# Reordered loads and step sizes at the start of a hybrid decoder step, and a reordered router

## The reference

```python
hp = rmsnorm(xp, norm_mix[i])
proj = h @ w_in                       # z | x, B, C | dt_raw
xbc = silu(conv(concat(conv_state, xbc)) + conv_b)       # width 4, per channel
dt = softplus(dt_raw + dt_bias); a = -exp(a_log)
y, h_last = ssd_scan(xs, dt, a, bm, cm, ssm_state)       # cumulative sums of dt * a over tokens
y = rmsnorm((y + xs * d_skip) * silu(z)) ; x = x + y @ w_out
...
grp = argmax(t @ w_route_group)                          # then the top 2 of the group's 8 experts
act = silu(gate) * up * combine ; out = out + act @ w_down
```

## Time and profile before

| | us |
|---|---|
| median of 3 runs | 1652.96 (1651.39 to 1654.72) |
| the profiled execution | 1652.1 |
| its span (first to last instruction) | 1650.3 |
| TensorE busy in the span | 1601.2 (97%) |
| VectorE busy | 619.9 (38%) |
| ScalarE busy | 449.0 (27%) |
| GpSimd busy | 142.2 (9%) |
| HBM traffic over the span | 328 GB/s |

### The profile page before, as it was taken

How to read it: one execution, slowest core, us unless ns; L and a number is a source line. 1 busy time by engine, 2 the same in 40 slices (tenths; PEclk the granted TensorE clock), 3 DMA queues, 4 the chain that set the end, 5 groups by cost and what they waited for, 6 DMA issues and landing times.

```text
span 1650.3 us, 21196 instructions
## 1 busy us (share of the span) xinstructions
PE 1601.2 (97%) x7929; PEld 934.2 (57%) x7929; DVE 619.9 (38%) x1356; ACT 449.0 (27%) x1168; POOL 142.2 (9%) x295
## 2 busy tenths in 40 slices
PE   9998879999999999999999999999999999999997
PEld 7877667653444344344877888877653444344342
DVE  4589993321322222123023544554421322222123
ACT  3488872211111111112143142232311111111112
POOL 1233341100000000001001202230000000000000
PEclk9999989999999999999999999999999999999999
DMA  9668777499999999999434956696599999999995
GB/s 340 204 212 264 219 237 286 151 400 401 427 428 424 429 428 424 430 425 399 175 132 162 331 183 239 173 275 285 226 401 402 429 426 425 429 427 426 430 424 214
DMA packets 107589, 542.24 MB, mean 329 GB/s; under 512 B 8780, under 2 KB 33556, under 8 KB 78546
## 3 DMA queue, kind: packets, MB, share of 16 engines
q1 hardware_dynamic: 90518, 485.20, 73.0%
q0 software_dynamic: 16672, 55.53, 10.7%
q10 hardware_dynamic: 316, 0.37, 0.1%
HBM read 524.81 MB, written 16.45 MB: 328 GB/s over the span
## 4 chain that ended last, share of the span: by engine, by line
PE 78%; DVE 10%; DMA 5%; ACT 4%; issue 2%; POOL 0%; SPq 0%; DVEq 0%; ACTq 0%
PE bank L1049 25%; PE bank L1413 14%; PE bank L1061 13%; PE bank L1032 5%; PE bank L1055 4%; PE bank L884 4%; DMA ring<-in_moe_w_gate_up 3%; PE bank L1344 3%; PE bank L1316 3%; DVE arena L2452 2%; PE bank L1642 2%; DVE arena L2297 2%; PE bank L1075 1%; ACT arena L1764 1%; DVE arena L2460 1%
## 5 line engine op out<-in xcount | busy, mean ns | idle before, releaser
L1049 PE MATMUL bank<-ring,arena 128*64 128x512 f32 x1520 | 335.7, 592 | 2.9 <-DMA ring<-in_moe_w_gate_up 2.8
L1413 PE MATMUL bank<-hT,ring 128*128 128x264 f32 x1152 | 269.4, 389 | 0.2
L1413 PEld LDWEIGHTS bank<-hT,ring 128*128 128x128 f32 x1152 | 214.4, 190 | 41.2 <-issue 3.9
L1049 PEld LDWEIGHTS bank<-ring,arena 128*64 128x64 f32 x1520 | 111.7, 137 | 214.4 <-issue 214.1
L2297 DVE TENSOR_TENSOR arena<-arena,bank 128x512 f32<-128x512 f32 x32 | 34.2, 1070 | 389.2 <-ACT arena L1764 389.2
L1061 PE MATMUL bank<-ring,arena 128*64 128x512 f32 x768 | 170.1, 595 | 1.6 <-DVE arena L2218 1.6
L1055 PE MATMUL bank<-arena 128*128 128x512 f32 x256 | 127.0, 618 | 1.6 <-ACT arena L1774 1.6
L1764 ACT ACTIVATE arena<-bank 128x512 f32<-128x512 f32 x32 | 19.1, 597 | 386.0 <-PE bank L1049 386.0
L2244 DVE SCALAR_TENSOR_TENSOR arena<-arena 128x1024 f32<-128x1024 f32 x32 | 41.1, 1284 | 213.2 <-ACT arena L1774 213.2
L1049 PE MATMUL bank<-arena 128*64 128x512 f32 x512 | 112.6, 592 | 0.0
L1061 PEld LDWEIGHTS bank<-ring,arena 128*64 128x64 f32 x768 | 53.8, 137 | 101.8 <-issue 99.7
(11 more groups left out here) (348 smaller groups left out, 1713.2 us busy)
## 6 DMA issues: line engine op xcount, KB each, us to landing
ring<-in_moe_w_gate_up SPq DMA_DIRECT2D x78, 2048.0 KB, 18.6
ring<-in_moe_w_down SPq DMA_DIRECT2D x48, 2048.0 KB, 23.6
arena<-in_moe_w_gate_up SPq DMA_DIRECT2D x32, 2048.0 KB, 18.9
ring<-in_attn_qkv SPq DMA_DIRECT2D x18, 2048.0 KB, 11.6
ring<-in_moe_w_gate_up SPq DMA_DIRECT2D x34, 1024.0 KB, 17.6
arena<-in_moe_w_down SPq DMA_DIRECT2D x32, 1024.0 KB, 21.2
ring<-in_ssm_in_proj SPq DMA_DIRECT2D x10, 2048.0 KB, 14.2
out<-arena POOLq DMA_DIRECT2D x24, 512.0 KB, 4.3
```

The source lines that it names most:

```text
L1049: mm = pe.matmul(bank[j][e * SLOTS:(e + 1) * SLOTS, :], Xg[:, 4 * half + k, 2 * (p % 2) + e, :], gate_rows(2 * half + e, p, k, first)[:, j ...
L1413: mm = pe.matmul(bank[i % 2][:, 0:T], wv[:, k, (i % 4) * P:(i % 4 + 1) * P], hT[:, k, :], start=(n == 0), stop=(n == DT - 1))
```

## The change

In the beginning: GpSimd's copy of old rows goes behind the first `old_columns`; ScalarE asks for the old rows only after its square roots; SyncE asks for the time-step weights behind chunk 1. TensorE's first constant products are four of 512 columns and two of 128; the vectors are turned first, then three parts of x, the scales, the other five. The old rows are turned behind tile 1, the step sizes are projected behind tile 2, ScalarE's part is at i = 2 and VectorE's five pieces behind `convolve(1)` to `convolve(5)`. `steps_to_tokens` stays behind tile 6.

In the routing: the constant products are four of 512 columns and three of 128 with the samples' turns between them, the rank products are merged (four records), one more long product follows them; ScalarE scales the samples' rows first; the counts come behind the gathers, and VectorE's use of them behind its last `first_tokens`; TensorE waits for the rounds ahead of the samples' weights.

```diff
--- before.py
+++ after.py
@@ -581,7 +581,7 @@
                     src = w_out[:, :, c:c + 256]
                     dst = ring[:, n % RING, :].rearrange("p (k n) -> p k n", k=16)
                 sp.dma_start(dst, src).then_inc(s_ld[n % RING], 16)
-                if n == 0:
+                if n == 1:
                     sp.dma_start(dtw[:, :, :], w_in[:, :, IN_DIM - SH:IN_DIM]).then_inc(s_aux, 16)
             for t in range(11, XT_TILES):
                 states_in(t)
@@ -649,9 +649,6 @@
                     pool.dma_start(wr[l][:, :, EG + EPG * g:EG + EPG * (g + 1)],
                                    a["moe_route_expert"][l, g].rearrange("(k p) e -> p k e", p=P)).then_inc(m_wr, 16)
-
-            pool.dma_start(conv_s[0, :, 0:2, :].rearrange("b w c -> b (w c)"),
-                           a["state_conv"][0, :, 1:3, :].rearrange("b w c -> b (w c)")).then_inc(s_pout, 16)
             link(pool.memset(ones[:, :], 1.0))
             pool.affine_select(out=ident[:, :], in_=ones[:, :], compare_op=ALU.is_equal, fill=0.0, base=0,
@@ -718,6 +715,9 @@
                 pool.tensor_copy(newc[:, ct, PADW:PADW + NS], new).then_inc(s_nc, 1)
             old_columns(0)
+            pool.dma_start(conv_s[0, :, 0:2, :].rearrange("b w c -> b (w c)"),
+                           a["state_conv"][0, :, 1:3, :].rearrange("b w c -> b (w c)")).then_inc(s_pout, 16)
+
             for i in range(PRE):
                 old_columns(i + 1)
                 new_columns(i)
@@ -888,6 +888,12 @@
                 for _ in range(n):
                     pe.matmul(bank[b][:, 3 * P:4 * P], ident[:, :], upper[:, :], start=True, stop=True)
+            def long_busy(b, n):
+
+                for _ in range(n):
+                    pe.matmul(bank[b][:, :], ident[:, :], upper[:, :].unsqueeze(1).to_broadcast([P, 4, P]),
+                              start=True, stop=True)
+
             def vectors():
                 pe.wait_ge(s_const, 4)
                 pe.wait_ge(s_vld, 112)
@@ -913,13 +919,13 @@
                 mm.then_inc(s_pvec, 1)
             def first_norm():
+                vectors()
                 pe.wait_ge(s_xld, 32)
-                for d in range(4):
+                for d in range(3):
                     turned(d, range(3)).then_inc(n_tp, 1)
-                vectors()
                 for i in range(2):
                     scales_spread(0, i)
-                for d in range(4, 6):
+                for d in range(3, 6):
                     turned(d, range(3)).then_inc(n_tp, 1)
                 pe.wait_ge(s_vvec, 6)
                 turned(7, range(3)).then_inc(n_tp, 1)
@@ -976,19 +982,24 @@
                 mm.then_inc(m_lg, 1)
                 pe.wait_ge(n_var, VAR_BASE[k] + 1)
-                busy(0, 19 - 4 * l)
-                pe.wait_ge(m_mk, 3 * l + 1)
-                for t in range(2):
-                    for u in range(t + 1):
-                        mm = pe.matmul(bank[0][:, (t + 1) * NE:(t + 2) * NE], (strict if u == t else ones)[:, :], msk[:, u, :],
-                                       start=(u == 0), stop=(u == t))
-                mm.then_inc(m_rk, 1)
-                pe.wait_ge(n_xn, XN_BASE[k] + 3)
+                long_busy(0, 2)
+                pe.wait_ge(n_xn, XN_BASE[k] + 1)
                 for d in range(DT):
                     transpose(bank[7][:, d * NS:(d + 1) * NS], xn_e[0:NS, 2, d * P:(d + 1) * P])
-                for u in range(2):
-                    mm = pe.matmul(bank[7][:, 2 * P:2 * P + NE], ones[:, :], msk[:, u, :], start=(u == 0), stop=(u == 1))
-                mm.then_inc(m_rk, 1)
+                long_busy(0, 2)
+                busy(0, 3)
+                pe.wait_ge(m_mk, 3 * l + 1)
+                pe.matmul(bank[0][:, NE:3 * NE], strict[:, :], msk[:, 0:2, :].rearrange("p t e -> p (t e)"),
+                          start=True, stop=False)
+                pe.matmul(bank[0][:, 2 * NE:3 * NE], ones[:, :], msk[:, 0, :], start=False, stop=True).then_inc(m_rk, 1)
+                long_busy(4, 1)
+                pe.wait_ge(n_xn, XN_BASE[k] + 3)
+
+                def token_counts():
+
+                    for u in range(2):
+                        mm = pe.matmul(bank[7][:, 2 * P:2 * P + NE], ones[:, :], msk[:, u, :], start=(u == 0), stop=(u == 1))
+                    mm.then_inc(m_rk, 1)
                 def chunk_landed(j, it, p):
@@ -1085,6 +1096,7 @@
                     mm.then_inc(m_rk, 1)
                 def sample_weights():
+                    pe.wait_ge(m_R, l + 1)
                     pe.wait_ge(m_mk, 3 * l + 2)
                     pe.matmul(bank[7][:, P:P + NE], sel8[0:NS, :, :].rearrange("p e s -> p (e s)"), cmb[0:NS, 2, :],
                               start=True, stop=True).then_inc(m_rk, 1)
@@ -1094,6 +1106,7 @@
                     if i == 3:
                         pe.wait_ge(s.xg, 1)
                     gather_pair(i, 0, (4, 5, 6, 4)[i]).then_inc(s.ga, 1)
+                token_counts()
                 pe.wait_ge(s_xa, 12 * l + 6)
                 def four(it, f, last=False, first=False):
@@ -1175,7 +1188,8 @@
                     scatter(j)
             pe.wait_ge(s_const, 2)
-            busy(6, 16)
+            long_busy(6, 4)
+            busy(6, 2)
             first_norm()
             def old_conv_rows():
@@ -1319,9 +1333,9 @@
             for i in range(PRE):
                 conv_tile(i)
-                if i == 0:
+                if i == 1:
                     old_conv_rows()
-                elif i == 1:
+                elif i == 2:
                     step_sizes()
                 elif i == 5:
                     new_columns(0)
@@ -1681,7 +1695,6 @@
                 if k == 0:
                     act.dma_start(head_v[0:SH, 0:1], a["ssm_dt_bias"].rearrange("l h -> h l")).then_inc(s_aux, 16)
                     act.dma_start(head_v[0:SH, 1:2], a["ssm_a_log"].rearrange("l h -> h l")).then_inc(s_aux, 16)
-                    act.dma_start(csr[0:CW * NS - NS, :], a["state_conv"][0].rearrange("b w c -> (b w) c")).then_inc(s_aux, 16)
                     act.wait_ge(s_xld, 32)
                 squares(k, 0, junk)
                 squares(k, 2, junk)
@@ -1689,6 +1702,8 @@
                 if k:
                     squares(k, 1, junk)
                 root(1)
+                if k == 0:
+                    act.dma_start(csr[0:CW * NS - NS, :], a["state_conv"][0].rearrange("b w c -> (b w) c")).then_inc(s_aux, 16)
                 for n, d in enumerate(NORM_TILES):
                     act.wait_ge(n_tp, TP_BASE[k] + n + 1)
                     act.activation(xT[:, d, :], bank[d][:, 0:T], ACT.Copy).then_inc(n_hs, 1)
@@ -1738,7 +1753,8 @@
                 act.wait_ge(m_ge, 3 * l + 1)
                 act.wait_ge(s_ot, 8 * l + 6)
-                for t, r in enumerate(ROWS):
+                for t in (2, 0, 1):
+                    r = ROWS[t]
                     for q in range(2):
                         ins = act.activation(xn_e[0:r, t, 512 * q:512 * q + 512].rearrange("r (k p) -> r k p", k=4),
                                              bank[(5, 1)[q] + t][0:r, :].rearrange("r (p k) -> r k p", k=4),
@@ -1867,7 +1883,7 @@
             for i in range(PRE + 1):
                 if i < PRE:
                     raw_copy(i)
-                if i == 1:
+                if i == 2:
                     step_sizes()
                 if i >= 2:
                     conv_silu(i - 2)
@@ -2245,11 +2261,6 @@
                                            in1=acc_s[:, :, :], op0=ALU.mult, op1=ALU.add).then_inc(s.ys, 1)
                 slots(slice(0, 4))
-                v.wait_ge(m_rk, 4 * l + 2)
-                link(v.tensor_reduce(cnt_s[0:1, 0:1], bank[7][0:1, 2 * P:2 * P + NE], AX, ALU.max))
-                link(v.tensor_scalar(cnt_s[0:1, 1:1 + ROUNDS], thresh[0:1, 0:ROUNDS], cnt_s[0:1, 0:1], None, ALU.is_lt))
-                link(v.tensor_reduce(cnt_s[0:1, 7:8], cnt_s[0:1, 2:1 + ROUNDS], AX, ALU.add))
-                v.tensor_copy(more_i[0:1, 0:1], cnt_s[0:1, 7:8]).then_inc(m_R, 1)
                 v.tensor_tensor(Xg[:, :, :, 0:NS], bank[7][:, 0:DT * NS].rearrange("p (d b) -> p d b", d=DT).unsqueeze(
                     2).to_broadcast([P, DT, 4, NS]), gffn_fours(l).unsqueeze(2).unsqueeze(3).to_broadcast([P, DT, 4, NS]),
                     ALU.mult)
@@ -2269,6 +2280,11 @@
                 by_group(cmb, e_in, NS, 2, 3).then_inc(m_mk, 1)
                 link(by_group(cmb, e_in, P, 0, 2))
                 first_tokens(3)
+                v.wait_ge(m_rk, 4 * l + 2)
+                link(v.tensor_reduce(cnt_s[0:1, 0:1], bank[7][0:1, 2 * P:2 * P + NE], AX, ALU.max))
+                link(v.tensor_scalar(cnt_s[0:1, 1:1 + ROUNDS], thresh[0:1, 0:ROUNDS], cnt_s[0:1, 0:1], None, ALU.is_lt))
+                link(v.tensor_reduce(cnt_s[0:1, 7:8], cnt_s[0:1, 2:1 + ROUNDS], AX, ALU.add))
+                v.tensor_copy(more_i[0:1, 0:1], cnt_s[0:1, 7:8]).then_inc(m_R, 1)
                 v.wait_ge(m_R, l + 1)
```

(4 more changed lines are left out.)

## The result

| | before | after |
|---|---|---|
| median of 10 runs each, us | 1652.99 (1651.39 to 1655.47) | 1657.82 (1656.13 to 1662.81) |
| ratio after/before, 95% interval | | 1.0031 [1.0021, 1.0041] |
| the profiled execution, its span | 1652.1, 1650.3 | 1656.13, 1654.4 |

The changed kernel is 0.31% slower: 4.8 us by the medians, 4.0 by the two profiled executions. The prediction said +5.1 us and 1658.1.

A forecast was written before the change was run, and what follows sets the result against it. The prediction took TensorE to bound the beginning and VectorE about 100 to 240 us. Start 0.2, stall 5.7, clock 0 and routing -0.8 sum to +5.1 us; 1652.96 + 5.1 = 1658.1 us, range 1653 to 1662.5.

The forecast's parts named there:

- The stall: At the turn to tokens behind tile 6, TensorE waits for step sizes ready only at 53.3 us: +5.7 us.
- The bounds given for it: Wait at the turn to tokens: 3.3 us if tile 0's activation doesn't hold convolution 2, 6.5 if VectorE has small gaps.
- It is passed on: After the turn to tokens, later tiles, sums, B and C queue behind TensorE's wait, so ScalarE, VectorE and POOL wait too.
- the rival of the absorbed stall: In the scan, TensorE idles for VectorE, so its late arrival costs nothing: 1652.4 us, chance 7%.
- The clock at that place: Behind the turn to tokens, the same clock loss as now: 0 net, -1.8 to +1.8 us.
- the rival in which the clock turns against the change: Layer 0's gathers stay cold, the restart at 53 us costs 1.8 more, vectors are late: 1661.5 us, chance 13%.
- The start: From warm-up to tile 0, warm-up and loads together: +0.5 - 0.3 = +0.2 us (0 to +2.4).
- The wait for the chunk: Ahead of tile 0, the first weight chunk lands sooner, which buys only TensorE's 0.27 us of waiting.
- the warm-up: TensorE's first constant products end 0.5 us later (0.3 to 1.2).
- The vectors in time: At the start TensorE reads the vectors at 10 us instead of 11.46; missing them would cost up to 1.5 us.
- The routing: Both layers' routing: layer 0 -1.2 us with gathers at full clock, layer 1 +0.4; sum -0.8 (-2.4 to +1.2).
- the marks that the prediction set: Profile signs: chunk before 14 us, 5 to 6 us idle before turns at about 53, convolution 2 at 37.7, gathers 3.8 us.

The follow-up runs named there:

- Experiment 2: The kernel before with only the new order (old rows behind tile 1, step sizes behind tile 2): 1663.46 us, ratio 1.0052.
- experiment 4: The changed kernel with TensorE's turn of the step sizes to tokens moved from behind tile 6 to behind tile 8: 1647.21 us, ratio 0.9964.
- experiment 3: The changed kernel with ScalarE's activation of tile 0 put ahead of its part of the step sizes: 1655.25 us, ratio 1.0006.
- experiment 6: The kernel before with all three loads late (copy, old rows, time-step weights), order of products as before: 1653.61 us, ratio 1.0002.
- experiment 7: The kernel before with the changed routing alone: 1650.66 us, ratio 0.9983.
- experiment 5: The kernel before with only GpSimd's copy of old rows put behind its first old columns: 1651.83 us, ratio 0.9997.
- experiment 12: experiment 4 with the counts' four products back between the ranks and the long product, VectorE's use of them late: 1646.99 us, ratio 0.9961.
- experiment 10: experiment 4 without the long product behind the ranks: 1647.65 us, ratio 0.9962.
- Experiment 9: experiment 4 with short products of the same total length replacing the long ones in both routers: 1650.85 us, ratio 0.998.
- experiment 1: The changed kernel with the old order of old rows and step sizes; late loads, early constants and new routing stay: 1652.74 us, ratio 0.9996.

## Why the prediction was right, and which terms were wrong

- **The stall (+5.7, measured 5.95): right, and so was its chain.** The sum's own terms give 5.9 (53.3 less 47.42); it put 5.7, because it moved only one side of the difference by the begin's 0.2. Experiment 2 has it alone, experiment 4 removes it by moving the reader, experiment 3 removes the part that tile 0's activation makes. The bounds given for it (3.3 without that activation) are what experiment 3 measured: 3.24.
- **It is passed on: right.** +7.31 behind tile 9, +6.99 at the end of the output projection. Only 0.3 us came back over the scan and the output projection, and the rival of the absorbed stall is refuted.
- **The clock at that place (0, measured +2.7): mis-sized.** The step "I take the same loss as now" was wrong. Before, the narrow products themselves ran at full clock (2.04 us) and only what followed was cold. With the gap they are cold as well (+1.56, turns +0.2) and tiles 7 to 9 lose 0.98 us more. The prediction let the cold stretch last some 5 us behind the gap, by the earlier trace rows, and set it against a loss of the same size; it lasted over 8 us, on top of narrow products that had lost nothing before. The loss of 1.8 us that it took as given is itself a draw: experiments 6 and 7, with the same narrow products at the same place, don't have it. Of the rival in which the clock turns against the change, the cold restart is the part that came true, and by more than its 1.8. The Trainium skill ("TensorE: Matmul & The Clock Gate", section "Why this matters for your kernels") warns of a gap that puts the clock back to half; the trace agrees, with 0.81 over the last 2 us of the gap and 0.50 for the 8 us behind it. In experiment 3 the gap of 3.24 us left the clock at 1.00, and it fell only behind the narrow products.
- **The start (+0.2, measured -1.43): mis-sized, and its sign wrong.** The sum costed the copy's transfer and not its issue on GpSimd. That issue stood ahead of the constants for which the first product waits: experiment 5 starts TensorE 1.24 us sooner by it alone. The wait for the chunk (0.27) went as said. From TensorE's start to tile 0 the changed kernel takes 0.08 us more than the kernel before without that wait, where the sum had +0.5 for the warm-up: -1.24 - 0.27 + 0.08 = -1.43.
- **The vectors in time: right in the changed kernel, not always.** TensorE waited 1.22 us for them in experiment 3's execution and 0.36 in experiment 12's; the bound of 1.5 held both.
- **The routing (-0.8): mis-sized.** The two traces give -1.41 and +0.2, but experiment 7 gives -2.8. The sum took layer 1's warm gathers as the rule; they were a draw. The reason was wrong too: by experiment 10 it isn't the product behind the ranks. What is left is the filler ahead of them (long products), the samples' turns, which now stand among it and no longer between ranks and gathers, and the merged ranks. Experiment 9 speaks for the long products by its median and its mean clock, but in its own trace the gathers are at full clock, so this is not shown.
- **The sum** came out near (+5.1 against +4.8) in part by luck, because errors met: 5.1 + 0.25 (stall) + 2.7 (clock) - 1.6 (start) - 0.4 (routing in these two traces) = 6.0 us. The scan took up 0.3 and the experts' stages gave back 1.7 that no term had, which leaves the 4.1 of the spans.

Of the marks that the prediction set, these were met: no DMA wait of tile 0 (that the chunk landed before 14 us isn't shown, as nobody waited for it; in experiment 6 it was there by 14.40), the idle time of 5 to 6 us released by VectorE's product, the order of the Silu table and convolution 2, the gathers at 3.8 us. The last piece ended at 51.93 us and not at 53.3, and the turns started at 51.99 and not at about 53, by the earlier start.

Open: in which stage experiment 9's slower executions lose their clock; what about the changed routing keeps it; what keeps tile 0 at full clock; and whether the 2.8 us of the routing come from the gathers alone, since no execution outside the profile shows its clock by stage.

## What to carry to other kernels

When a producer is moved a step later in hand-written order, list its readers on every engine and move those that have no slack: here the last piece was ready 0.3 us ahead of its reader, and moving it by one tile cost 5.95 us of gap and 2.7 us of clock, while moving the reader by two tiles as well took both away and made the kernel 0.36% faster than before. Loads that are asked for later want later readers, and one that shares a semaphore with another is as late as the later of both: in experiment 1 the old rows were there by 16 us and were turned at 21.28. A cold or warm stretch in one trace is one draw: look for it in several executions before it enters a sum.

## What the runs showed of the hardware

- Tile 0, which comes behind the warm-up and some 6.5 us of turning, was at full clock (16 records in 3.83 us) in 9 of the 14 kernels' profiled executions and at half in the other five (6.25 to 6.74 us; 9.30 and 9.65 for tiles 0 and 1 together). That is 2.3 to 2.9 us more for the same records.
- Narrow products without any gap can be followed by half clock: before, 64 of 16 columns took 2.04 us at full clock and the 3 us behind them ran at 0.50. The same products at the same place had full clock behind them in experiments 6 and 7 (48 records in 10.95 us):

```profile
50.55 10.95 PE L1317 MATMUL bank<-hT,ring 128*128 128x264 f32 x48
```

- Within experiment 9 the executions with a lower mean granted clock are the longer ones: 0.995 or 0.996 up to 1647.65 us and 0.991 to 0.994 from 1648.52 us on.
- The granted clock's column says 1.00 in the warm-up, though its records came every 0.203 us before and every 0.119 in the router. The two don't agree there, and a sum should go by the records' durations.
- The slow stretch of the weight stream moves with the load of the old rows (24 rows of 12 KB, asked for at 9.19 us in the changed kernel, its packets at 12 to 16 us): 199 GB/s at 9 to 10 us before, and after (stretch, busy PE, PEld, DVE, ACT, POOL, clock, DMA share, GB/s)

```profile
9.00:10.00 1.00, 1.00 (x8) 0.69 (x7) 0.68 (x5) 0.24 (x2) 0.00 (x0) 1.00 1.06 397
...
14.00:15.00 1.00, 1.00 (x7) 0.72 (x6) 1.00 (x4) 0.73 (x3) 0.00 (x0) 1.00 0.81 164
```
